# Sixteen filter taps of one convolution tile as diagonal products on TensorE, and the decay factors of two units made on ScalarE

## The chip, the cores and the metric

One core of one Trainium2 chip runs the kernel. The metric is the device time of one execution in microseconds, and the time of a kernel is the median of its runs. PE is TensorE, DVE is VectorE, ACT is ScalarE, SP is the queue that issues most transfers, and PSUM is the memory with eight banks into which PE writes.

## What is computed

One inference step of one decoder layer: a mixer with two groups of heads (an SSD group and a convolution group) that share an input and an output projection, then a mixture of 32 experts with four chosen for each token. There are 272 prompt tokens (16 of them learned, in front) and 8 sample tokens, of width 1024, all in float32. What matters for the change is this part of the mixer:

```python
val, gate = jnp.split(glu_in, 2, axis=-1)
c = val * jax.nn.sigmoid(gate)
c, conf_hist_new = causal_dwconv(c, conf_hist, conv_conf_w, conv_conf_b)   # 31 taps per channel
...
a_cum = jnp.cumsum(dt * a.astype(F32).reshape(g, r), axis=2)
seg = a_cum[:, :, :, None] - a_cum[:, :, None, :]
decay_ls = jnp.exp(jnp.where(causal, seg, -jnp.inf))
cb = jnp.einsum('bclgn,bcsgn->bclsg', cm, bm)
y_diag = jnp.einsum('bclsg,bclsgr,bcsgrp->bclgrp', cb, decay_ls, xdt)
decay_to_end = jnp.exp(a_cum[:, :, -1:] - a_cum)
chunk_decay = jnp.exp(a_cum[:, :, -1])
```

## The kernel before, in words

Channels lie on the 128 partitions, tokens along the free dimension. The order of the work on each engine is the order in which the code is written; semaphores are the only ties between engines.

**PE** makes the input projection in 36 tiles of 128 output channels, each of eight products (`w_in_tiles`, line 1214): 16 for the convolution group, 12 for the SSD group, and 8 Z tiles for the output gate. Z tiles 3 to 7 stand between the steps of the scan. Each tile goes to a PSUM bank that `tile_bank` names, and waits until the bank's former tile has been read; for Z tiles 4 to 7 that is ACT, which applies SiLU to each Z tile (`z_tiles`, line 510, semaphore `z_out`).

**The long convolution** (`wide_conv`, line 696) lies on DVE: eight tiles of 256 tokens with 31 taps each. ACT makes tap 0, and DVE the 30 others, one scalar-multiply-add over a 128x256 tile each, 240 in all. They are dealt out in 90 rounds: rounds 0 to 29 treat tiles 0 and 1 (two taps a round), rounds 30 to 59 tiles 2 and 3, and rounds 60 to 89 tiles 4 to 7, four taps a round. The rounds are laid as filling between steps of other work.

**The scan** handles two chunks of 128 tokens and two groups of eight heads, so four units `u`. For a unit, `exponents` (line 771) subtracts `acum` from the row sums and caps at zero, head by head (eight instructions on DVE), into `Mh[u]`; `decays` (lines 471 and 472) takes the exponential of `Mh[u]` and of the row sums `Ce[u]` on ACT; `unit_factors` (lines 826 to 830) on DVE copies the last column of each to `dec_u` and `cdec_u` and multiplies them by `cbm` and by C. Then PE's `unit` (lines 1257 and 1259) makes the outputs (`y_mm`), waits for `xdec` of DVE (line 852), and makes the new state (line 1263, `st_mm`). DVE waits for `y_mm` at line 861 and for `st_mm` at line 866. Rows of a chunk are transposed by PE (line 1190) and taken over by DVE (`rows_of_chunk`, lines 819 and 821).

**What follows**: after the last round DVE drains and releases `conv_done` (line 870), for which PE waits with the mean of the layer norm (line 1314). Beside this SP loads the output weights once Z tile 7 is done (line 272), the sample states once unit 3's output is done (line 278), and, after DVE's `dtx` has been written to DRAM and is back, its broadcast rows (line 310). DVE's `decode` (lines 875 and 880) uses both, and ahead of the output projection (line 1303) stands the norm (DVE line 901, ACT line 547). The experts follow, with their weights streamed from HBM.

Of the kernel before, what the change touches and what calls it, by code (L numbers as in the profile page):

```python
# [9 lines left out]
ACT = mybir.ActivationFunctionType  # L10
AX = mybir.AxisListType.X

P = 128
D = 1024
KT = D // P
# [32 lines left out]
def build(nc, I, O):  # L48
    ctx = ExitStack()
    with ctx:  # L50
# [52 lines left out]
        Mh = [view(ring, at, HPG, P) for at in (2112, 3136, 12288, 13312)]  # L103
        Ce = [view(ring, 8192 + D * u, HPG, P) for u in range(4)]
# [97 lines left out]
        names = ("rowsum_ready rowsum_out rowsum_landed tap_added narrow_added decay_done consts x_lo x_hi vec_loaded sq_a sq_v stat_mm xr_ready uT_ready win_done gsig_ready glu_done csmp_loaded xsmp_loaded "  # L202
# [27 lines left out]
        def tile_bank(j):  # L230
            if j >= Z_TILE:
                return 4 + j - Z_TILE if j < Z_TILE + 2 else 3 * (j % 2)
            return j % 6
# [187 lines left out]
        def _(a):  # L421
# [47 lines left out]
            def decays(u):  # L469
                a.wait_ge(ev["d_ready"], u + 1)  # L470
                act(flat(Mh[u]), flat(Mh[u]), ACT.Exp).then_inc(ev["e_ready"], 1)
                act(flat(Ce[u]), flat(Ce[u]), ACT.Exp).then_inc(ev["ce_ready"], 1)
# [25 lines left out]
            for x in range(XT_):  # L498
                narrow_first(x)
                if x >= 3 and x % 2:  # L500
                    narrow_silu(x - 3)
                    narrow_silu(x - 2)
# [164 lines left out]
        def _(v):  # L667
# [15 lines left out]
            tap_no = {}  # L683
            for q_ in range(ROUNDS):
                for m_ in CONV_SETS[q_ // NR]:
                    tap_no[m_, 1 + q_ % NR] = len(tap_no) + 1

            def wide_conv(first, last):
                for q in range(first, last):
                    tiles, k = CONV_SETS[q // NR], 1 + q % NR  # L690
                    if k == 1:
                        v.wait_ge(ev["ctap_ready"], tiles[-1] + 1)
                    for m in tiles:
                        if k > 1:
                            v.wait_ge(ev["tap_added"], tap_no[m, k - 1])
                        STT(conv[:, m, 0:SEQ], cbuf[:, m, k:k + SEQ], cw[:, m, k:k + 1], conv[:, m, 0:SEQ], ALU.mult, ALU.add  # L696
                            ).then_inc(ev["tap_added"], 1)
# [115 lines left out]
            exponents(2)  # L813
            exponents(3)

# [7 lines left out]
            def unit_factors(u):  # L823
                c, g_ = u // 2, u % 2
                v.wait_ge(ev["ce_ready"], u + 1)
                V.tensor_copy(dec_u[u], Mh[u][:, :, P - 1])
                V.tensor_copy(cdec_u[u], Ce[u][:, :, P - 1])
                v.drain()
                TT(Mh[u], Mh[u], bc(cbm[:, u, :], 1, HPG), ALU.mult)
                TT(Ce[u], Ce[u], bc(xa[:, 10 + g_, 16 + c * P:16 + (c + 1) * P], 1, HPG), ALU.mult).then_inc(ev["m_ready"], 1)  # L830
# [7 lines left out]
            TT(cbm, ps[:, 4, :].rearrange("p (u t) -> p u t", u=4), bc(tri, 1, 4), ALU.mult)  # L838
# [30 lines left out]
            wide_conv(UNIT_R[3][2], ROUNDS)  # L869
            v.drain().then_inc(ev["conv_done"], 1)  # L870
# [314 lines left out]
        def _(pe):  # L1185
# [12 lines left out]
            def w_in_tiles(first, last):  # L1198
                for j in range(first, last):
# [3 lines left out]
                    if j >= Z_TILE + 4:  # L1203
                        pe.wait_ge(ev["z_out"], j - Z_TILE - 1)
# [60 lines left out]

            w_in_tiles(Z_TILE, Z_TILE + 3)
# [14 lines left out]
            w_in_tiles(Z_TILE + 4, Z_TILE + 5)  # L1281
            unit(0)
            chunk_rows(2, META + P, P)
            w_in_tiles(Z_TILE + 5, Z_TILE + 6)
            unit(1)
            w_in_tiles(Z_TILE + 6, Z_TILE + 7)
            unit(2)
            w_in_tiles(Z_TILE + 7, Z_TILE + 8)
            unit(3)
# [484 lines left out]
```

## Time and profile before

| | us |
|---|---|
| median of 3 runs | 1303.73 (1300.33 to 1305.13) |
| profiled execution, its own time | 1293.74 |
| its span in the trace | 1291.9 |
| busy in the span: PE, DVE, ACT | 1165.0, 495.7, 184.7 |

The span is what the trace covers; 1.8 us of the profiled execution lie around it. "Busy" is an average over stages with different limits, so the stages are what has to be read: the mixer ends at about 300 us, and the remaining 992 us are the experts. A row of a timeline gives the start in us, the time from the first start to the last end of the merged instructions, the engine, line, operation, operands, their count, and in brackets how long the engine was idle before and what released it. Each matmul in float32 shows as two records.

### The profile page before, as it was taken

To read this page: it belongs to the slowest core of one execution; us is meant where nothing else is said; L and a number is where in the kernel's file an instruction comes from. 1 tells how busy PE (TensorE), PEld (TensorE's weight loads), DVE (VectorE), ACT (ScalarE), POOL (GpSimd) and SP (SyncE) were. 2 spreads that over 40 slices of the span, in tenths; PEclk is the share of its full clock that TensorE was granted. 3 is DMA by queue.
4 is the path that set the end of the run, shared out by engine and by line. 5 is a ranking of instruction groups with operands and counts; after the bars stand their busy time and mean duration, and the time that the engine had idled before them with its cause. 6 is when DMAs were issued, how large, how long until landed. Compare 5 with 4: busy or idle time off the path is not lost.

```text
span 1291.9 us, 21086 instructions
## 1 busy us (share of the span) xinstructions
PE 1165.0 (90%) x8422; PEld 547.0 (42%) x8423; DVE 495.7 (38%) x1117; ACT 184.7 (14%) x391; POOL 4.6 (0%) x28
## 2 busy tenths in 40 slices
PE   7999878997998989999989999899999887989886
PEld 5888657873333333333333433233433323323323
DVE  2799998303423322133322232322232332323233
ACT  2132304012111110011100011100111111101011
POOL 0000000000000000000000000000000000000000
PEclk9999988998989999999999999999999999989897
DMA  9541309723799999899999899998999999999993
GB/s 395 200 178 65 139 3 328 280 123 143 308 427 425 428 429 429 324 421 429 429 428 417 332 421 430 429 427 360 395 420 428 430 428 428 428 429 429 428 428 154
DMA packets 36995, 451.33 MB, mean 349 GB/s; under 512 B 5112, under 2 KB 5656, under 8 KB 10080
## 3 DMA queue, kind: packets, MB, share of 16 engines
q1 hardware_dynamic: 35344, 449.02, 83.4%
q10 hardware_dynamic: 1616, 1.82, 0.4%
q8 instruction: 25, 0.41, 0.1%
q14 instruction: 10, 0.08, 0.0%
HBM read 443.57 MB, written 7.25 MB: 349 GB/s over the span
## 4 chain that ended last, share of the span: by engine, by line
PE 57%; DMA 28%; DVE 12%; issue 2%; DVEq 1%; ACT 0%; SPq 0%; ACTq 0%
DMA ring<-in_w_experts 27%; PE ps L1419 24%; PE ps L1462 9%; DVE acts L696 6%; PE ps L1214 3%; PE ps L1303 2%; PE ps L1396 2%; PE ps L1360 2%; PE ps L1429 2%; PE ps L1471 2%; PE ps L1190 2%; DVE acts L791 1%; PE ps L1294 1%; PE ps L1409 1%; PE ps L1452 1%
## 5 line engine op out<-in xcount | busy, mean ns | idle before, releaser
L1419 PE MATMUL ps<-ring,extra 128*64 128x512 f32 x1824 | 418.4, 603 | 13.8 <-DMA ring<-in_w_experts 13.8
L1053 DVE TENSOR_TENSOR acts<-ps,acts 128x528 f32<-128x528 f32 x128 | 90.6, 708 | 398.7 <-PE ps L1429 200.2
L1462 PE MATMUL ps<-ring,extra 128*32 128x256 f32 x3072 | 204.7, 403 | 40.4 <-DMA ring<-in_w_experts 38.1
L1419 PEld LDWEIGHTS ps<-ring,extra 128*64 128x64 f32 x1824 | 123.0, 137 | 262.8 <-issue 232.3
L1462 PEld LDWEIGHTS ps<-ring,extra 128*32 128x32 f32 x3072 | 90.8, 114 | 144.9 <-DMA ring<-in_w_experts 57.4
L696 DVE SCALAR_TENSOR_TENSOR acts<-acts,small 128x256 f32<-128x256 f32 x240 | 97.8, 482 | 0.7 <-ACT acts L451 0.7
L1214 PE MATMUL ps<-acts,ring 128*128 128x280 f32 (+1 forms) x320 | 76.4, 398 | 0.0
L1214 PEld LDWEIGHTS ps<-acts,ring 128*128 128x128 f32 x320 | 61.7, 194 | 15.1 <-issue 2.1
L1214 PE MATMUL ps<-acts,extra 128*128 128x280 f32 x256 | 62.7, 408 | 1.9 <-DVE acts L681 1.9
L1067 DVE TENSOR_SCALAR extra<-ps 128x512 f32<-128x512 f32 x32 | 22.0, 689 | 97.7 <-PE ps L1419 82.4
L1396 PE MATMUL ps<-acts 128*64 128x512 f32 (+1 forms) x228 | 56.6, 616 | 0.0
L1214 PEld LDWEIGHTS ps<-acts,extra 128*128 128x128 f32 x256 | 49.6, 194 | 14.5 <-issue 2.3
L590 ACT ACTIVATE extra<-extra 128x512 f32<-128x512 f32 x32 | 19.7, 630 | 237.1 <-DVE extra L1058 237.1
L1190 PE MATMUL ps<-small,extra 128*128 128x128 f32 x220 | 38.9, 290 | 14.4 <-DVE extra L1072 13.0
L1429 PE MATMUL ps<-acts,extra 64*128 64x264 f32 x304 | 51.1, 426 | 0.0
L1090 DVE SCALAR_TENSOR_TENSOR acts<-ps,acts 128x264 f32<-128x264 f32 x48 | 22.2, 490 | 63.3 <-ACT acts L620 63.1
L1471 PE MATMUL ps<-acts,extra 32*128 32x264 f32 x256 | 46.2, 437 | 0.0
L1190 PEld LDWEIGHTS ps<-small,extra 128*128 128x128 f32 x220 | 22.8, 140 | 48.6 <-issue 20.8
L585 ACT ACTIVATE extra<-ps 128x512 f32<-128x512 f32 x34 | 20.4, 601 | 152.7 <-PE ps L1396 142.0
L1040 DVE TENSOR_SCALAR extra<-ps 128x256 f32<-128x256 f32 x16 | 6.8, 424 | 91.7 <-PE ps L1462 91.7
L1471 PEld LDWEIGHTS ps<-acts,extra 32*128 32x128 f32 x256 | 19.3, 184 | 53.4 <-issue 53.4
L600 ACT ACTIVATE extra<-ps 128x512 f32<-128x512 f32 x32 | 17.4, 594 | 129.4 <-PE ps L1419 129.4
(284 smaller groups left out, 870.4 us busy)
## 6 DMA issues: line engine op xcount, KB each, us to landing
ring<-in_w_experts SPq DMA_DIRECT2D x192, 2048.0 KB, 21.6
ring<-in_w_in_t SPq DMA_DIRECT2D x5, 2048.0 KB, 20.8
extra<-in_w_in_t SPq DMA_DIRECT2D x4, 2048.0 KB, 10.4
extra<-in_w_out_t SPq DMA_DIRECT2D x4, 1024.0 KB, 6.2
ring<-in_w_out_t SPq DMA_DIRECT2D x4, 1024.0 KB, 5.9
ring<-in_state_t SPq DMA_DIRECT2D x8, 512.0 KB, 8.1
ring<-dtx_rows SPq DMA_DIRECT2D x8, 512.0 KB, 6.3
out_ssm_s_t<-ring SPq DMA_DIRECT2D x8, 512.0 KB, 5.2
```

The costliest lines, as they stand in the source:

```text
L696: STT(conv[:, m, 0:SEQ], cbuf[:, m, k:k + SEQ], cw[:, m, k:k + 1], conv[:, m, 0:SEQ], ALU.mult, ALU.add).then_inc(ev["tap_added"], 1)
L1053: TT(both, ps[:, 6:8, 0:TN], both, ALU.add).then_inc(ev["acc_done"], 1)
L1090: return STT(Pm[:, bank, :], ps[:, 6, 0:TN], slot_id[:, slot:slot + 1], gp, ALU.is_equal, ALU.mult)
L1190: return nc.tensor.transpose(out, in_, ident[0:r, 0:r])
L1214: h = MM(ps[:, tile_bank(j), 0:T - lo], win(c)[:, k, P * q:P * (q + 1)], uT[:, k, lo:T], start=(k == 0), stop=(k == KT - 1))
L1303: h = MM(ps[:, m, 0:TN], wout(4 + k // 2)[:, k % 2, P * m:P * (m + 1)], conv[:, k, :], start=(k == 0), stop=False, skip_group_check=True)
L1360: h = MM(ps[:, m, 0:TN], wout(k // 2)[:, k % 2, P * m:P * (m + 1)], yT[:, k, :], start=False, stop=(k == KT - 1), skip_group_check=True)
L1396: h = MM(dst, S[0:r, j, HALF * b:HALF * (b + 1)], xn[0:r, j, 512 * h_:512 * (h_ + 1)], start=(j == 0), stop=(j == 2))
L1419: hs.append(MM(dst, src[:, o:o + HALF], piece(p)[:, k, 512 * h_:512 * (h_ + 1)], start=(fresh and kk == 0), stop=(kk == KT - 1), skip_grou ...
L1429: h = MM(ps[:, 6 + h_, 0:TN], ys[rows, 512 * b + P * m:512 * b + P * (m + 1)], Pm[rows, b, :], start=(b == 0), stop=(b == n - 1))
L1462: hs.append(MM(dst, src[:, o:o + QUAR], piece(p)[:, k, 256 * q:256 * (q + 1)], start=(fresh and kk == 0), stop=(kk == KT - 1), skip_group_ ...
L1471: h = MM(ps[:, 6 + h_, 0:TN], ys[QUAR * q:QUAR * (q + 1), P * (m % 2):P * (m % 2 + 1)], Pm[QUAR * q:QUAR * (q + 1), 0, :], start=True, sto ...
```

## The change

The last convolution tile (tile 7) keeps taps 1 to 14 on DVE. Its taps 15 to 30 become sixteen products on PE: ACT makes sixteen 128x128 diagonal matrices of the tap weights while the SSD group's convolution runs, PE multiplies each with the shifted 128x256 input and accumulates all in PSUM bank 3, in pieces of 5, 4, 4 and 3 behind Z tiles 4 to 7, and DVE adds the bank to tile 7 at the end, ahead of `conv_done`. So that bank 3 is free, Z tiles 4 to 7 all go to bank 0, and each waits for ACT's reading of the one before it.

`exponents` for units 2 and 3 leave DVE: ACT makes them with Relu in `decays`, eight instructions a unit, and takes the sign into the scale of the exponential. The last columns of all four units are copied on ACT behind the exponentials. `unit_factors` loses its copies and the drain, and multiplies `Ce` first, then `Mh`.

```diff
+        PE_TILE, PE_TAP, PE_TAPS = KT - 1, CW - 16, 16
+        diag = view(ring, 14336, PE_TAPS, P)
...
         def tile_bank(j):
             if j >= Z_TILE:
-                return 4 + j - Z_TILE if j < Z_TILE + 2 else 3 * (j % 2)
+                return (4, 5, 0, 3, 0, 0, 0, 0)[j - Z_TILE]
...
             def decays(u):
-                a.wait_ge(ev["d_ready"], u + 1)
-                act(flat(Mh[u]), flat(Mh[u]), ACT.Exp).then_inc(ev["e_ready"], 1)
-                act(flat(Ce[u]), flat(Ce[u]), ACT.Exp).then_inc(ev["ce_ready"], 1)
+                if u < 2:
+                    a.wait_ge(ev["d_ready"], u + 1)
+                    act(flat(Mh[u]), flat(Mh[u]), ACT.Exp)
+                else:
+                    for k in range(HPG):
+                        act(Mh[u][:, k, :], Ce[u][:, k, :], ACT.Relu, scale=-1.0, bias=acum[:, u // 2, HPG * (u % 2) + k:HPG * (u % 2) + k + 1])
+                    a.drain()
+                    act(flat(Mh[u]), flat(Mh[u]), ACT.Exp, scale=-1.0)
+                act(flat(Ce[u]), flat(Ce[u]), ACT.Exp)
+                a.drain()
+                act(dec_u[u], Mh[u][:, :, P - 1], ACT.Copy)
+                act(cdec_u[u], Ce[u][:, :, P - 1], ACT.Copy).then_inc(ev["ce_ready"], 1)
...
                 narrow_first(x)
+                if x >= XT_ - PE_TAPS // 2:
+                    for j in (2 * (x - XT_) + PE_TAPS, 2 * (x - XT_) + PE_TAPS + 1):
+                        act(diag[:, j, :], ident, ACT.Identity, scale=cw[:, PE_TILE, PE_TAP + j:PE_TAP + j + 1]).then_inc(ev["diag_ready"], 1)
...
-                    for m in tiles:
+                    for m in [t for t in tiles if not on_pe(t, k)]:
...
-            exponents(2)
-            exponents(3)
...
             def unit_factors(u):
                 c, g_ = u // 2, u % 2
                 v.wait_ge(ev["ce_ready"], u + 1)
-                V.tensor_copy(dec_u[u], Mh[u][:, :, P - 1])
-                V.tensor_copy(cdec_u[u], Ce[u][:, :, P - 1])
-                v.drain()
-                TT(Mh[u], Mh[u], bc(cbm[:, u, :], 1, HPG), ALU.mult)
-                TT(Ce[u], Ce[u], bc(xa[:, 10 + g_, 16 + c * P:16 + (c + 1) * P], 1, HPG), ALU.mult).then_inc(ev["m_ready"], 1)
+                TT(Ce[u], Ce[u], bc(xa[:, 10 + g_, 16 + c * P:16 + (c + 1) * P], 1, HPG), ALU.mult)
+                v.wait_ge(ev["cbm_ready"], 1)
+                TT(Mh[u], Mh[u], bc(cbm[:, u, :], 1, HPG), ALU.mult).then_inc(ev["m_ready"], 1)
...
             wide_conv(UNIT_R[3][2], ROUNDS)
+            v.wait_ge(ev["taps_mm"], 1)
+            v.wait_ge(ev["tap_added"], tap_no[PE_TILE, PE_TAP - 1])
+            TT(conv[:, PE_TILE, 0:SEQ], conv[:, PE_TILE, 0:SEQ], ps[:, 3, 0:SEQ], ALU.add)
             v.drain().then_inc(ev["conv_done"], 1)
...
                     if j >= Z_TILE + 4:
-                        pe.wait_ge(ev["z_out"], j - Z_TILE - 1)
+                        pe.wait_ge(ev["z_out"], 3 if j == Z_TILE + 4 else j - Z_TILE)
...
+            def pe_taps(first, last):
+                if first == 0:
+                    pe.wait_ge(ev["z_out"], 4)
+                    pe.wait_ge(ev["diag_ready"], PE_TAPS)
+                for j in range(first, last):
+                    h = MM(ps[:, 3, 0:SEQ], diag[:, j, :], cbuf[:, PE_TILE, PE_TAP + j:PE_TAP + j + SEQ],
+                           start=(j == 0), stop=(j == PE_TAPS - 1), skip_group_check=True)
+                return h
...
             w_in_tiles(Z_TILE + 4, Z_TILE + 5)
+            pe_taps(0, 5)
             unit(0)
             chunk_rows(2, META + P, P)
             w_in_tiles(Z_TILE + 5, Z_TILE + 6)
+            pe_taps(5, 9)
             unit(1)
             w_in_tiles(Z_TILE + 6, Z_TILE + 7)
+            pe_taps(9, 13)
             unit(2)
             w_in_tiles(Z_TILE + 7, Z_TILE + 8)
+            pe_taps(13, PE_TAPS).then_inc(ev["taps_mm"], 1)
             unit(3)
```

On DVE, from the end of the SSD group's convolution to the first unit's factors, this stands before (771 is `exponents`, 696 the taps, 826 to 830 `unit_factors(0)`):

```order
L811 TENSOR_TENSOR acts<-acts,small 128x12x8
L771 TENSOR_SCALAR ring<-ring,small 128x128 x16
L696 SCALAR_TENSOR_TENSOR acts<-acts,small 128x256 [waits tap_added] x4
L819 TENSOR_TENSOR ring<-ps,small 16x512 [waits xtok_mm]
L819 TENSOR_TENSOR ring<-ps,small 16x512
L821 COPY ring<-ps 16x256
L836 TENSOR_TENSOR ring<-ring,small 16x1024 [waits meta_exp]
L838 TENSOR_TENSOR small<-ps,small 128x512 [waits cb_mm]
L826 COPY small<-ring 128x8 [waits ce_ready]
L827 COPY small<-ring 128x8
L829 TENSOR_TENSOR ring<-ring,small 128x1024
L830 TENSOR_TENSOR ring<-ring,acts 128x1024
```

and this with the change (713 is the taps, 840 and 842 `unit_factors(0)`):

```order
L828 TENSOR_TENSOR acts<-acts,small 128x12x8
L713 SCALAR_TENSOR_TENSOR acts<-acts,small 128x256 [waits tap_added] x3
L833 TENSOR_TENSOR ring<-ps,small 16x512 [waits xtok_mm]
L833 TENSOR_TENSOR ring<-ps,small 16x512
L835 COPY ring<-ps 16x256
L848 TENSOR_TENSOR ring<-ring,small 16x1024 [waits meta_exp]
L850 TENSOR_TENSOR small<-ps,small 128x512 [waits cb_mm]
L840 TENSOR_TENSOR ring<-ring,acts 128x1024 [waits ce_ready]
L842 TENSOR_TENSOR ring<-ring,small 128x1024 [waits cbm_ready]
```

Sixteen instructions, one tap and two copies are gone from this piece; the rest keeps its order but for the two products of `unit_factors`.

On PE, behind unit 2, this stands before (1214 is Z tile 7, 1257 and 1259 are unit 3's output, 1263 its state, 1190 transposes, 1314 the mean):

```order
L1263 MATMUL ps<-ring 128x512 [waits hT_ready,xdec_ready]
L1214 MATMUL ps<-acts,ring 128x264 [waits z_out]
L1214 MATMUL ps<-acts,ring 128x264 x7
L1257 MATMUL ps<-ring 64x128 [waits hT_ready,y_ready,m_ready,xdt_ready]
L1257 MATMUL ps<-ring 64x128
```

and this with the change (1229 is Z tile 7, 1286 the taps, 1272 the start of unit 3's output):

```order
L1278 MATMUL ps<-ring 128x512 [waits hT_ready,xdec_ready]
L1229 MATMUL ps<-acts,ring 128x264 [waits z_out]
L1229 MATMUL ps<-acts,ring 128x264 x7
L1286 MATMUL ps<-acts,ring 128x256 x3
L1272 MATMUL ps<-ring 64x128 [waits hT_ready,y_ready,m_ready,xdt_ready]
L1272 MATMUL ps<-ring 64x128
```

Three of the sixteen new products now stand between Z tile 7 and unit 3; the other thirteen stand in the same way behind Z tiles 4, 5 and 6.

On ACT, between Z tile 3's SiLU and Z tile 4's, two loads of a table and four exponentials of 128x1024 (lines 471 and 472) stood before; now it is this (477 is the Relu, 479 and 480 the exponentials, 482 and 483 the copies, 524 the SiLU of Z tiles 4 to 7):

```order
L477 ACTIVATE ring<-ring,small 128x128 x8
L479 ACTIVATE ring<-ring 128x1024
L480 ACTIVATE ring<-ring 128x1024
L482 ACTIVATE small<-ring 128x8
L483 ACTIVATE small<-ring 128x8
L477 ACTIVATE ring<-ring,small 128x128 x8
L479 ACTIVATE ring<-ring 128x1024
L480 ACTIVATE ring<-ring 128x1024
L482 ACTIVATE small<-ring 128x8
L483 ACTIVATE small<-ring 128x8
L428 ACT_TABLE_LOAD
L524 ACTIVATE ring<-ps 128x264 [waits win_done] x4
```

Sixteen Relu and four copies have come in ahead of the SiLU of Z tile 4, and nothing there waits for DVE any more.

## Rows read from the trace of the kernel before

**Rows 1.** Windows: busy us (instructions) of PE, PEld, DVE, ACT, POOL; granted clock, DMA share, GB/s.

```profile
57.00:140.00 83.00, 82.28 (x352) 66.48 (x350) 82.67 (x214) 24.37 (x66) 0.24 (x1) 1.00 0.40 149
140.00:201.00 61.00, 43.22 (x267) 32.83 (x268) 58.24 (x138) 10.43 (x15) 0.00 (x0) 0.87 0.21 82
300.00:1292.00 992.00, 894.08 (x7059) 330.08 (x7059) 289.72 (x615) 113.55 (x242) 0.00 (x0) 0.97 0.94 397
```

**Rows 2.** Waits, 137 to 260 us: engine, line, releaser: us in total, times, longest.

```profile
PE ps L1257 <- DVE ring L821: 5.0, 1, 5.0
PE ps L1263 <- DVE ring L852: 4.9, 2, 2.7
PE ps L1314 <- DVEq L870: 4.5, 1, 4.5
PE ps L1278 <- DVE ring L836: 3.1, 1, 3.1
DVE ring L866 <- PE ps L1263: 0.8, 1, 0.8
DVE acts L861 <- PE ps L1259: 0.8, 1, 0.8
```

**Rows 3.** Timeline of DVE in the scan.

```profile
141.31 3.30 DVE L771 TENSOR_SCALAR ring<-ring,small 128x128 f32<-128x128 f32 x16
...
154.67 0.42 DVE L821 COPY ring<-ps 128x256 f32<-128x256 f32 x1
155.00 0.16 DVE L826 COPY small<-ring 128x8 f32<-128x8 f32 x1
...
155.31 1.23 DVE L829 TENSOR_TENSOR ring<-ring,small 128x1024 f32<-128x1024 f32 x1
...
197.21 3.25 DVE L696 SCALAR_TENSOR_TENSOR acts<-acts,small 128x256 f32<-128x256 f32 x8
```

**Rows 4.** Timeline of PE: unit 0, a state, a Z tile, a variance.

```profile
157.51 0.44 PE L1257 MATMUL ps<-ring 128*64 128x128 f32 x4
...
159.09 0.39 PE L1259 MATMUL ps<-ring 128*64 128x128 f32 x4
...
161.68 1.13 PE L1263 MATMUL ps<-ring 128*128 128x512 f32 x2 [2.20 <-DVE ring L852]
...
188.63 3.73 PE L1214 MATMUL ps<-acts,ring 128*128 128x264 f32 x16
...
206.78 3.62 PE L1319 MATMUL ps<-acts,small 128*128 128x256 f32 x16
```

**Rows 5.** Timeline of ACT.

```profile
84.61 0.60 ACT L451 ACTIVATE acts<-acts,small 128x256 f32<-128x256 f32 x1 [0.86 <-DVE acts L706]
...
86.53 0.28 ACT L476 ACTIVATE small<-ps 128x128 f32<-128x128 f32 x1
...
146.47 1.28 ACT L426 ACT_TABLE_LOAD   x1
147.76 1.06 ACT L471 ACTIVATE ring<-ring 128x1024 f32<-128x1024 f32 x1
```

**Rows 6.** Windows of PE alone: busy us (records), granted clock, DMA share, GB/s.

```profile
159.00:162.00 3.00, 0.80 (x11) 1.00 0.00 0
169.00:171.50 2.50, 0.36 (x8) 1.00 0.00 0
171.50:175.00 3.50, 2.96 (x5) 0.51 0.00 0
182.00:188.50 6.50, 5.35 (x34) 0.50 0.00 0
```

**Rows 7.** Timeline behind the scan: output weights, mean, broadcast rows, first decode.

```profile
192.39 0.81 SPq L272 DMA_DIRECT2D ring<-in_w_out_t  x2
...
200.65 6.29 PE L1314 MATMUL ps<-acts,small 128*128 128x264 f32 x16 [4.47 <-DVEq L870]
...
207.23 1.76 SPq L310 DMA_DIRECT2D ring<-dtx_rows  x4
...
211.19 1.41 DVE L880 SCALAR_TENSOR_TENSOR ring<-ring,acts 128x512 f32<-128x512 f32 x2 [0.65 <-DMA ring<-dtx_rows]
```

More of the change, by code:

```diff
@@ L199, in build @@
         lgT = view(acts, 5016, TN)
-        names = ("rowsum_ready rowsum_out rowsum_landed tap_added narrow_added decay_done consts x_lo x_hi vec_loaded sq_a sq_v stat_mm xr_ready uT_ready win_done gsig_ready glu_done csmp_loaded xsmp_loaded "
+        names = ("cbm_ready diag_ready taps_mm rowsum_ready rowsum_out rowsum_landed tap_added narrow_added decay_done consts x_lo x_hi vec_loaded sq_a sq_v stat_mm xr_ready uT_ready win_done gsig_ready glu_done csmp_loaded xsmp_loaded "
                  "dt_mm dt_v dt_exp dt_ready ctap_ready conv_done xtap_ready xtail_out xconv_done xs_pre xa_ready z_out "
@@ L683, in _, with on_pe @@
             tap_no = {}
+            def on_pe(m, k):
+                return m == PE_TILE and k >= PE_TAP
             for q_ in range(ROUNDS):
-                for m_ in CONV_SETS[q_ // NR]:
+                for m_ in [t for t in CONV_SETS[q_ // NR] if not on_pe(t, 1 + q_ % NR)]:
                     tap_no[m_, 1 + q_ % NR] = len(tap_no) + 1
@@ L837, in _ @@
             v.wait_ge(ev["cb_mm"], 1)
-            TT(cbm, ps[:, 4, :].rearrange("p (u t) -> p u t", u=4), bc(tri, 1, 4), ALU.mult)
+            TT(cbm, ps[:, 4, :].rearrange("p (u t) -> p u t", u=4), bc(tri, 1, 4), ALU.mult).then_inc(ev["cbm_ready"], 1)
             unit_factors(0)
```

## The prediction

> **What bounds the kernel now.** I began with the windows by stage [rows 1]. From 57 to 140 us DVE is busy 82.67 of 83 us, from 140 to 201 us 58.24 of 61, while PE has 43.22 of 61 and a clock of 0.87 on average, and ACT 10.43. So up to the end of the scan DVE is the bound. Behind 300 us the transfers are (0.94 busy); the change touches nothing there. The list of waits [rows 2] says the same from the other side: in the scan it is PE that waits for DVE, 5.0 us at unit 2, 4.9 us for two states, 3.1 us for the first state's factors and 4.5 us for `conv_done`. DVE waits for PE only twice, 0.8 and 0.8 us, both in unit 2. The reader is to see that an instruction taken from DVE in this stretch moves the end of the scan, and that one given to PE first fills a pause.
>
> The clock matters here [rows 6]. Unit 2 runs at 0.50, that is 1.2 GHz, after the pause of 5.0 us before it. The pause before the state at 161.68 was 2.20 us and the clock stayed at 1.00 (2.4 GHz); a pause of 2.7 us later [rows 2] was followed by 0.51. So a pause of 2.2 us has left the clock high once, one of 2.7 us has not.
>
> **The change part by part.**
>
> *Exponents of units 2 and 3.* Sixteen instructions leave DVE: 3.30 us from first start to last end [rows 3], of which 3.2 us are its own, since the next starts a little ahead of an end. Gain 3.2 us.
>
> *Taps.* Eight taps take 3.25 us from first start to last end, and each goes on 0.395 us behind the former [rows 3]. Sixteen leave: 6.3 us. They are one in the last step of the SSD convolution, one before the first rows, and fourteen inside the scan. With three tiles a round a tap still has two others between itself and its predecessor; with two tiles a round, early in the kernel, DVE was full as well [rows 1], so no new pause arises.
>
> *Copies and drain.* From the first copy (155.00) to the product (155.31) are 0.31 us [rows 3], four times: 1.2 us. The new waits on `ce_ready` and `cbm_ready` are looked at with ACT below; `cbm` is DVE's own work, one product earlier.
>
> *The addition at the end.* Not in the trace. Nearest are the copy of 128x256 from PSUM, 0.42 us, and half of the 128x1024 product's 1.23 us, 0.6 us [rows 3]. I take 0.4 and keep 0.6 as the upper end; it cannot gain. PE has made `taps_mm` before unit 3, whose output DVE has waited for, so it never waits.
>
> Sum on DVE: 3.2 + 6.3 + 1.2 - 0.4 = 10.3 us.
>
> *Sixteen products on PE.* A product of 128x256 is two of the sixteen records that take 3.62 us, so 0.43 us [rows 4]. Sixteen are 6.9 us. At half the clock it is 0.86 us, and that is the other bound; below 0.43 it will not be, since the shape is the same. Follow PE: the 3.1 us pause before the first state vanishes, because its factors are ready 4 us earlier and Z tile 3 ends later than they do. From there to unit 2 PE is nearly without a pause: in unit 0 the five products (2.2 us) and the output (157.51 to 159.48, 1.97 us [rows 4]) end before `xdec` is wanted, and unit 1 with four (1.7 us) ends some 2.7 us before DVE asks for it. Before unit 2 it waits for the rows of chunk 2, now about 1.8 us instead of 5.0 (the four products fill 1.7, and the earlier DVE takes the rest). That is shorter than the 2.20 us that left the clock high. I take the high clock for unit 2. Then its output takes 1.97 and its state 1.13 us instead of 3.7 and 2.0, and both waits of DVE in unit 2 end: a gain of 1.6 us that is no part of the DVE sum.
>
> In unit 3 the opposite happens. From the end of unit 2's state PE has Z tile 7 (3.73 us), three products (1.3) and the output (1.97): 7.0 us. DVE from there: it reaches the state about 0.4 us later (it now comes second), then 0.6 for line 866, six taps 2.4, `xdec` and `hT2` 1.3, three taps 1.2: 5.9 us. DVE waits 1.0 us.
>
> Sum at `conv_done`: 10.3 + 1.6 - 1.0 = **10.9 us**.
>
> *ACT.* The sixteen diagonals stand in a stretch where ACT is busy 24.37 of 83 us [rows 1], each behind the `narrow_first` that DVE waits for: hidden. If that cover were gone each pair would cost about 0.6 us. The decays of units 2 and 3 start with the table at about 146.0 + 0.1 us. A Relu of 128x128 with one operand per partition is not in the trace. Above lies 0.60 us for 128x256 with two such operands, below 0.28 for 128x128 with none [rows 5]; I take 0.37 alone and 0.28 in a row (an overlap of 0.09, as DVE's instructions at 154.67 and 155.00 show [rows 3]). Eight are 2.3 us, two exponentials 2.0 (1.06 the first), copies and drains 0.4: 4.7 us a unit. So unit 2 is ready at 147.4 + 4.7 = 152.1, unit 3 at 156.8; DVE asks for them at about 158 and 167 on the new time: it came to them at 163.7 and 174.1, and has by then gained 3.2 (exponents), 0.6 and 0.9 (copies) and five and eight taps (2.0 and 3.2). Then the table (1.28) and Z tile 4's SiLU (0.4) end at 158.5, and PE wants bank 0 for Z tile 5 at 158.8: from the end of Z tile 3 (145.9) two first states 1.8, transposes 1.1, Z tile 4 3.7, five products 2.2, unit 0's 1.97 and 1.13, transposes 1.1. This fits just; behind it lie the 2.7 us by which unit 1 is early. At 0.51 us a Relu (the 0.60 row less the overlap) it ends 3.7 us later, PE is late by 3.4, and DVE loses 1 to 1.6 us. Z tiles 6 and 7 find the bank long free: they are 8 us or more apart and SiLU takes 0.4.
>
> The Trainium skill speaks against this move: "ScalarE: Activation LUTs", section "Rules for kernel authors", tells to use VectorE for relu, max and min. Per instruction the trace agrees, 3.2 us on DVE against some 4.5 on ACT. By that rule alone the move would lose 1.3 us; by the rows it wins 3.2, because ACT has the time and DVE hasn't.
>
> *Does it reach the end?* `conv_done` is one way into the tail, the transfers the other. The broadcast rows were issued at 207.23, after `dtx` came back from DRAM behind the output weights (from 192.39) and the states, and DVE's first decode waited 0.65 us for them at 211.19 [rows 7]. That queue starts when Z tile 7 is done. With the change Z tile 7 ends at about 181.4 instead of 192.3: DVE has the rows of chunk 2 ready 8.4 us earlier (3.2, copies 1.2, ten taps 4.0), and unit 2 at the high clock saves 2.6. So this way moves by about 11 us too. Both move alike, and everything behind hangs on them in order; expert weights are first fetched when the states are done. So 10.9 us arrive. The mean at 200.65 took 6.29 us for the sixteen records after a 4.47 us pause; at the high clock it would take about 3.5. The pause will be some 2.5 us. Either way the decode behind it waits for the rows, so this gives only 0 to 0.65 us, and I take 0.
>
> **Sum**: 1293.74 - 10.9 = 1282.8 us for an execution like the profiled one, -0.84%. That execution was 0.8% faster than the median of the runs, 1303.73; the same share off the median gives **1292.8 us**.
>
> **Rivals.**
> 1. *PE becomes the bound.* If the clock stays low through the products (0.86 us each, units at 3.7), PE is late in units 1, 2 and 3 by 0.9, 2.0 and 2.7 us. For it speaks the mean clock of 0.87 and 0.51 after short pauses [rows 1, 6]; against it, that all its pauses become shorter. The gain falls to about 6.4 us: 1297.3. Chance 0.12. (Only unit 2 low: 9.2 us of gain, 1294.5, within the forecast.)
> 2. *The tail gives more.* The mean is at 2.4 GHz and the rows' transfers, less crowded, come earlier as well. Up to 2.8 us more: 1290.0. For it, the 2.5 us pause lies between the two seen; against it, the 0.65 us wait. Chance 0.14.
> 3. *The gain does not reach the end.* Something behind 300 us, where transfers are 0.94 busy for 992 us [rows 1], starts at a time the mixer does not set. Against it: the weights' first fetch waits for the sample states. 1303.7. Chance 0.08.
> 4. *Slower: ACT holds bank 0.* The two units' sixteen Relu stand ahead of Z tile 4's SiLU, for which Z tile 5 waits, and unit 1 and all taps behind it wait with it. PE may be late 2.7 us for free; the sign turns when the delay exceeds 2.7 + 10.9 = 13.6 us, that is 0.85 us more per Relu, 1.1 us each. At 1.3 us each it is 2.7 us slower: 1306.5. No row of 128 columns comes near [rows 5]. Chance 0.04.
> The forecast itself holds 0.62.
>
> **Numbers.** About 0.5% (6.5 us, below 1297.2) is what a measurement tells from no change. The forecast with its bounds (addition 0.2, Relu 1.6, unit 2's clock 1.7) is 1292.5 to 1296.5, and the runs of before spread by 2.5 us around their median; with rivals 1 and 2 in it the range is 1289 to 1298. Faster: 0.62 + 0.14 + half of rival 1 = 0.82; same 0.06 + 0.08 = 0.14; slower 0.04.
>
> **What the new profile would show.** DVE without line 771's sixteen in the scan and taps in threes and sixes; no pause of PE before the first state; no wait of DVE in unit 2 and about 1.0 us for `y_mm` in unit 3; products of 0.43 us; Relu of about 0.28 us apart; Z tile 5 hardly waiting for `z_out`; `conv_done` near 189.6. The forecast is wrong if a Relu takes over 0.5 us, if DVE waits for PE in units 1 and 2, or if the first broadcast rows land less than 10 us earlier.

## The result, and the profile after

| | before | after |
|---|---|---|
| median of the runs taken together | 1304.43 us (4) | 1286.84 us (4) |
| lowest to highest | 1300.33 to 1305.66 | 1283.26 to 1288.3 |
| profiled execution: time, span | 1293.74, 1291.9 | 1288.3, 1286.5 |

The ratio is 0.9873, with a 95% interval of 0.9845 to 0.9901: the kernel is 1.3% faster, by 17.6 us in these medians of four. The forecast of 1292.8 us (1289 to 1298) had the direction and missed the size; the median lies 2.2 us below the range. The two profiled executions differ by 5.4 us only, so the first question is where each stands among its kind.

The windows by stage of after, as in [rows 1], cut at the start of the scan, at `conv_done` and at 300 us:

```profile
57.00:141.50 84.50, 84.46 (x368) 68.31 (x366) 82.25 (x213) 29.22 (x85) 0.24 (x1) 1.00 0.42 158
141.50:191.10 49.60, 44.13 (x298) 34.45 (x298) 48.16 (x99) 16.27 (x36) 0.00 (x0) 1.00 0.25 95
191.10:300.00 108.90, 101.16 (x529) 82.77 (x531) 44.79 (x100) 27.14 (x57) 2.35 (x12) 0.93 0.63 237
300.00:1286.00 986.00, 895.17 (x7041) 327.12 (x7037) 284.07 (x588) 110.84 (x233) 0.00 (x0) 0.96 0.94 397
```

The scan takes 49.6 us where it took 61.0, DVE is still the bound in it (48.16 busy), and PE's clock is 1.00 from end to end, where it was 0.87.

The waits from 130 to 260 us, to be held against [rows 2]:

```profile
DVE ring L895 <- DMA ring<-dtx_rows: 3.2, 1, 3.2
...
PE ps L1342 <- DVEq L885: 2.7, 1, 2.7
...
PE ps L1272 <- DVE ring L835: 1.9, 1, 1.9
...
DVE acts L873 <- PE ps L1274: 0.7, 1, 0.7
...
PE ps L1229 <- ACT ring L524: 0.3, 1, 0.3
```

PE's four rows in [rows 2] add up to 17.5 us; in the same places, with Z tile 5 added, 4.9 are left. The wait before the first state and those for `xdec` are gone, the one before unit 2 went from 5.0 to 1.9 us, the one for `conv_done` from 4.5 to 2.7. (Behind `conv_done` PE has a new wait of 1.6 us in all, for DVE's decode.) DVE no longer waits in unit 2 and waits 0.7 us in unit 3 (forecast 1.0). Z tile 5 waited 0.3 us for bank 0 (forecast: it just fits).

The timelines of DVE, PE and ACT in the scan, for [rows 3 to 5]:

```profile
143.11 1.27 DVE L713 SCALAR_TENSOR_TENSOR acts<-acts,small 128x256 f32<-128x256 f32 x3
...
172.68 2.46 DVE L713 SCALAR_TENSOR_TENSOR acts<-acts,small 128x256 f32<-128x256 f32 x6
...
186.55 1.12 DVE L873 SCALAR_TENSOR_TENSOR acts<-acts,small,ps 128x128 f32<-128x128 f32 x4 [0.72 <-PE ps L1274]
...
190.58 0.42 DVE L884 TENSOR_TENSOR acts<-acts,ps 128x256 f32<-128x256 f32 x1
```

```profile
154.38 2.32 PE L1286 MATMUL ps<-acts,ring 128*128 128x256 f32 x10
...
161.03 3.83 PE L1229 MATMUL ps<-acts,ring 128*128 128x264 f32 x16 [0.29 <-ACT ring L524]
...
191.17 3.80 PE L1342 MATMUL ps<-acts,small 128*128 128x264 f32 x16 [2.73 <-DVEq L885]
```

```profile
149.57 2.45 ACT L477 ACTIVATE ring<-ring,small 128x128 f32<-128x128 f32 x8
152.09 1.06 ACT L479 ACTIVATE ring<-ring 128x1024 f32<-128x1024 f32 x1
```

Taps come in threes and sixes, the addition (L884) takes 0.42 us, and no `exponents` stand in the scan. Five products take 2.32 us, 0.46 each with the overlap. Eight Relu take 2.45 us, 0.30 apart. The mean (L1342) takes 3.80 us instead of 6.29, at a granted clock of 1.00.

The tail on DVE, for [rows 7]:

```profile
197.34 1.22 DVE L890 TENSOR_TENSOR ring<-ring,small 128x1024 f32<-128x1024 f32 x1
201.73 1.41 DVE L895 SCALAR_TENSOR_TENSOR ring<-ring,acts 128x512 f32<-128x512 f32 x2 [3.17 <-DMA ring<-dtx_rows]
```

The wait for the broadcast rows grew from 0.65 to 3.17 us: what the mean gave, this wait took.

### The profile page after: what moved, and what is told of

The parts are those of the page before. It is cut to its first block, busy times and chain, and to the rows that moved or that the text cites. A ratio compares the mean times of both kernels' runs of the same rounds, so it can differ in the third digit from the quotient of the medians.

```text
span 1286.5 us, 21155 instructions
## 1 busy us (share of the span) xinstructions
PE 1173.8 (91%) x8454; PEld 551.2 (43%) x8455; DVE 485.5 (38%) x1078; ACT 195.5 (15%) x431; POOL 4.6 (0%) x28
## 4 chain that ended last, share of the span: by engine, by line
PE 55%; DMA 30%; DVE 12%; issue 1%; DVEq 1%; ACT 0%; SPq 0%; ACTq 0%
DMA ring<-in_w_experts 29%; PE ps L1447 24%; PE ps L1490 8%; DVE acts L713 5%; PE ps L1229 3%; PE ps L1331 2%; PE ps L1424 2%; PE ps L1388 2%; PE ps L1499 2%; PE ps L1457 2%; PE ps L1205 2%; DVE acts L808 1%; PE ps L1322 1%; PE ps L1437 1%; PE ps L1480 1%
## 5 line engine op out<-in xcount | busy, mean ns | idle before, releaser
L1447 PE MATMUL ps<-ring,extra 128*64 128x512 f32 x1824 | 426.3, 613 | 15.3 <-DMA ring<-in_w_experts 15.3
L713 DVE SCALAR_TENSOR_TENSOR acts<-acts,small 128x256 f32<-128x256 f32 x224 | 91.3, 477 | 0.7 <-ACT acts L453 0.7
L1082 DVE TENSOR_SCALAR extra<-ps 128x512 f32<-128x512 f32 x32 | 22.0, 688 | 97.8 <-PE ps L1447 82.5
L1424 PE MATMUL ps<-acts 128*64 128x512 f32 (+1 forms) x228 | 56.6, 616 | 0.0
L1457 PE MATMUL ps<-acts,extra 64*128 64x264 f32 x304 | 51.2, 427 | 0.0
```

What stands on the lines that cost most here:

```text
L1424: h = MM(dst, S[0:r, j, HALF * b:HALF * (b + 1)], xn[0:r, j, 512 * h_:512 * (h_ + 1)], start=(j == 0), stop=(j == 2))
L1447: hs.append(MM(dst, src[:, o:o + HALF], piece(p)[:, k, 512 * h_:512 * (h_ + 1)], start=(fresh and kk == 0), stop=(kk == KT - 1), skip_grou ...
L1457: h = MM(ps[:, 6 + h_, 0:TN], ys[rows, 512 * b + P * m:512 * b + P * (m + 1)], Pm[rows, b, :], start=(b == 0), stop=(b == n - 1))
```

## Stages of all traces

To see where executions differ I took six marks in each trace: the start of the scan (DVE's 128x384 product, 141.43 in after), the 128x64 product behind `conv_done` (191.11), DVE's first addition of the output projection (255.82), the first and the last gate of the experts with few tokens, and the last output. "Start" is the time of DVE's first copy of the row sums. The table gives the distances in us, and under it every experiment refers to it. The last column gives the span. The columns do not add up to it: from "start" to the scan it is 82.9 us in before and 82.5 in after, and from the last gate to the end 35 to 37.

| trace | start | scan | to the projection's first sum | to the first gate | experts | span |
|---|---|---|---|---|---|---|
| before, the one shown | 56.7 | 61.0 | 63.4 | 90.4 | 900.7 | 1291.9 |
| before, again | 56.5 | 60.9 | 65.7 | 94.4 | 900.5 | 1297.9 |
| before, a third | 58.9 | 60.8 | 66.2 | 96.6 | 903.6 | 1304.8 |
| before, a fourth | 56.5 | 60.9 | 63.9 | 91.7 | 901.1 | 1292.6 |
| after, the one shown | 58.9 | 49.7 | 64.7 | 91.8 | 902.0 | 1286.5 |
| after, again | 56.4 | 49.7 | 65.4 | 91.7 | 900.5 | 1282.3 |
| after, a third | 56.8 | 49.7 | 65.1 | 92.1 | 901.9 | 1283.3 |
| decays only | 56.8 | 55.2 | 62.9 | 91.7 | 900.0 | 1285.4 |
| taps only | 56.8 | 56.1 | 65.9 | 91.9 | 901.2 | 1290.0 |
| products unread | 56.2 | 61.0 | 66.5 | 92.0 | 901.3 | 1295.7 |
| four times Relu | 56.1 | 64.7 | 66.6 | 92.1 | 901.5 | 1298.9 |
| after + 1.1 us | 56.8 | 49.9 | 64.4 | 93.4 | 901.1 | 1282.9 |
| after + 2.0 us | 56.4 | 49.7 | 63.1 | 93.6 | 900.1 | 1284.2 |
| after + 3.4 us | 56.9 | 51.2 | 66.3 | 100.7 | 900.9 | 1297.2 |
| before + 1.3 us | 59.0 | 62.6 | 65.7 | 94.4 | 900.1 | 1301.8 |
| before + 2.65 us | 56.1 | 59.4 | 62.4 | 91.7 | 901.5 | 1292.1 |
| before + 3.4 us | 56.5 | 60.8 | 63.1 | 90.4 | 898.6 | 1291.9 |
| after, filled | 56.6 | 49.7 | 65.4 | 90.2 | 899.0 | 1279.2 |
| before, filled | 55.3 | 62.4 | 67.7 | 89.6 | 902.2 | 1296.4 |
| after + 1.1, filled | 56.9 | 49.9 | 66.7 | 91.5 | 899.4 | 1285.4 |

In the four traces of before and the three of after the scan is 60.8 to 61.0 and 49.7 us: 11.1 to 11.3 us shorter whichever two are compared. On the mean the spans differ by 12.8 us: 11.2 in the scan, 0.4 ahead of it, 1.2 from the scan's end to the first gate, and nothing in the experts. That last stretch goes with PE's granted clock in it: in before it took 153.8, 155.6, 160.1 and 162.8 us at a clock of 0.94, 0.93, 0.90 and 0.90, in after 156.5, 157.1 and 157.2 us at 0.93, 0.92 and 0.92.

Before's scan is not always the same, though. "Before, filled" has its edit behind the scan and yet a scan of 62.4 us. In it the clock fell already in the products of the first state (0.53 from 148 to 152 us), and DVE waited 1.44 us for the rows of chunk 1. PE in before, then PE and DVE in "before, filled":

```profile
149.16 1.95 PE L1278 MATMUL ps<-ring 16*128 16x512 f32 x4 [3.13 <-DVE ring L836]
```

```profile
147.78 3.32 PE L1278 MATMUL ps<-ring 16*128 16x512 f32 x4 [3.14 <-DVE ring L836]
...
153.46 1.29 DVE L819 TENSOR_TENSOR ring<-ps,small 128x512 f32<-128x512 f32 x2 [1.44 <-PE ps L1190]
```

## Experiments

**Both kernels again**, with more executions.

> The kernel before, unchanged, as a control. Open question: the medians of before and after lie 17.6 us apart, but 10.9 us were forecast and the two traces show 11.2 us less from the sample convolution (before 139.71, after 141.51 us) to the end of the wide convolution, and their spans differ by 5.4 us only. Theory A (variation): executions of one kernel differ by several us outside the scan (clock at the start, expert stage), the extra 6.7 us is such variation, and this control comes out within 3 us of the kernel before with a scan of 60.8 us in its trace. Theory B (real): the scan before normally takes longer than in the one trace shown (pauses fall differently against the clock), so that this trace, if its time is near 1303, shows the scan 4 to 8 us longer than 60.8 us.

> The changed kernel, unchanged, timed in more rounds. Theory A: the difference to before shrinks towards 11 us (8 to 14). Theory B: it stays at 15 to 20 us.

Measured: before 1300.9 us (12 executions, 1295.56 to 1306.62), after 1285.4 (6, 1284.09 to 1288.02), 0.9898 [0.9849, 0.9947] against the runs of before beside it. Against the 1299.6 of before beside it, after is 14.2 us faster, between the 8 to 14 of theory A and the 15 to 20 of theory B; the scan of before is 60.9 us in its trace, so the long scan of theory B did not show. The first median of before was high by chance: 123 executions of it beside the experiments have a median of 1299.98, from 1291.22 to 1310.41; 16 of after have 1286.15, from 1283.26 to 1291.45. The difference is thus about 13.8 us, not 17.6 (95% of the differences lie between 12.6 and 15.8 when both sets of executions are drawn anew, with repetition, many times).

**Each half alone.** The one kernel is after without `on_pe`, diagonals, `pe_taps` and the bank table; the other is after with the decays as before:

```diff
-                return m == PE_TILE and k >= PE_TAP
+                return False
```

```diff
+            exponents(2)
+            exponents(3)
...
+                V.tensor_copy(dec_u[u], Mh[u][:, :, P - 1])
+                V.tensor_copy(cdec_u[u], Ce[u][:, :, P - 1])
+                v.drain()
```

> Only the decay part: exponents of units 2 and 3 and the copies of all units on ACT, all thirty taps of tile 7 on DVE, banks as before. By the sum of the prediction DVE loses 3.2 and 1.2 us of work: the end of the wide convolution 4.4 us earlier, and up to 2.6 us more if unit 2 runs at 2.4 GHz (its pause stays near 5 us, so I expect 1.2 GHz there): 1299 to 1300 us. Theory B: 6 us or more.

> Only the taps: sixteen products on PE, exponents and copies stay on DVE. By the sum: 6.3 less 0.4 us of DVE work, 1.6 us if unit 2 comes to run at 2.4 GHz (its pause falls to about 2.8 us), 1.0 us lost in unit 3: 5 to 7 us, 1297 to 1299. Theory B: 9 us or more.

Measured: decays alone 1293.04 (0.9967 [0.993, 1.0004]), taps alone 1293.07 (0.995 [0.9917, 0.9982]). Their scans are 5.8 and 4.9 us shorter, 10.7 together; both at once give 11.3. In medians they give some 7 us each against 1299.98, and 13.8 together. Both times lie below their ranges by the sum (1299 to 1300, 1297 to 1299), but the median of before was still uncertain, and the interval of decays alone reaches from no gain to 9 us: that each half gives more than its scan is not shown. With taps alone DVE waits 1.63 us for the rows of chunk 1, which are late at a low clock as in "before, filled". With decays alone PE still waits 6.1 us before unit 2, and unit 2 meets the low clock, as was expected: its first four records take 0.69 us, where they take 0.44 in after:

```profile
178.58 0.69 PE L1269 MATMUL ps<-ring 128*64 128x128 f32 x4 [6.10 <-DVE ring L835]
```

By the Trainium skill ("ScalarE: Activation LUTs", section "Rules for kernel authors", use VectorE for relu) `exponents` belongs on DVE. Per instruction the traces agree: 0.20 us apart on DVE [rows 3], 0.30 on ACT. The stage decides otherwise: with this half alone, copies included, the scan is 5.8 us shorter, because DVE was busy for 58.24 of 61 us and ACT for 10.43 [rows 1].

**The products alone.** Before, with the diagonals and the sixteen products in their places, while DVE makes all taps itself and nobody reads bank 3:

```diff
             w_in_tiles(Z_TILE + 4, Z_TILE + 5)
+            pe_taps(0, 5)
             unit(0)
```

> The kernel before, in which ACT also makes the sixteen diagonals and PE the sixteen products in their new places, with the new banks, but DVE still adds all taps itself and reads none of the products. DVE has the same work as before. What the products can do here is fill PE's pauses. Clock theory (the extra gain is that PE no longer falls to 1.2 GHz in the scan, and that this fall varies from run to run before): faster than before by 1.5 to 5 us, no DVE wait in unit 2, and runs that spread less than before's 19 us. Plain sum theory (all gain is DVE work removed, the rest of the difference lies behind the scan by chance): no change or up to 1.3 us slower, and the spread of before.

Measured: 1299.62, 0.9985 [0.9961, 1.0009], scan 61.0, as by the plain sum theory. The products cost nothing and bring nothing that can be told from noise: some 7 us of PE's work lie in pauses. PE still waits 4.67 us before unit 2, and the clock in the scan is 0.89 instead of 0.87; with the taps gone from DVE it is 0.91, with both halves 1.00.

**Relu four times over**, to see whether ACT can hold bank 0 (rival 4):

```diff
+                    for _ in range(4):
+                        for k in range(HPG):
+                            act(Mh[u][:, k, :], Ce[u][:, k, :], ACT.Relu, ...)
```

> The changed kernel with the eight Relu of units 2 and 3 done four times each (same result, a drain behind each pass), so that ACT reaches the SiLU of Z tile 4 about 14.8 us later. By the rival on ACT: PE waits some 15 us for the bank at Z tile 5, 2.7 us of that free, and the scan grows by 12 us, from 49.7 to about 62, the time of before or a little more. If Z tile 5 were not what matters, but only the decays themselves, units 2 and 3 would have them 7.4 and 14.8 us later against leads of about 5 and 9 us: 5 to 6 us lost.

Measured: 1303.4, 1.0023 [0.9996, 1.0049], scan 64.7: all of the gain is lost. The timeline of PE shows the chain that rival 4 describes, and that of DVE who pays. (DVE also waits 2.04 and 3.39 us for the late decays of units 2 and 3, but behind these it still waits for PE, so the bank sets the end.)

```profile
173.32 5.71 PE L1230 MATMUL ps<-acts,ring 128*128 128x264 f32 x16 [15.37 <-ACT ring L525]
```

```profile
182.71 1.12 DVE L874 SCALAR_TENSOR_TENSOR acts<-acts,small,ps 128x128 f32<-128x128 f32 x4 [8.74 <-PE ps L1275]
```

The 48 added Relu are 14.6 us (0.305 each, from the eight in 2.45), and rival 4 put the turn of the sign at 13.6: with a median just above before's, that fits. Its mechanism is real; only the Relu is not slow. Its price was too low: the scan grew by 15.0 us where 12 were expected, and behind the pause the Z tile took 5.71 us instead of 3.83, at a clock of 0.70 from 173 to 180 us.

**Single traces of before.** Two more of them, so that its spread can be seen by stage.

> The kernel before, one more look. The 29 runs of before spread from 1291 to 1310 us, the changed kernel's from 1283 to 1288. If the scan causes the spread, a run over 1303 shows it longer than 61 us with half clock in units 0, 1 or 3; if not, the scan is 61 us again and the difference lies in the experts or in their start.

> The same once more, for a second point: scan 61 us whatever the time, or longer with the time.

Measured: 1306.62 and 1294.43. The table shows 12.2 us of span between them, and none in the scan: 2.4 at the start, 2.3 ahead of the projection's first sum, 4.9 ahead of the first gate, 2.5 in the experts. Two groups of eight products behind the routing, and a window of PE alone, in the slower:

```profile
327.86 3.68 PE L1419 MATMUL ps<-ring,extra 128*64 128x512 f32 x8
...
332.65 3.68 PE L1419 MATMUL ps<-ring,extra 128*64 128x512 f32 x8
320.00:330.00 10.00, 9.01 (x38) 0.65 0.01 2
```

and in the faster:

```profile
322.50 1.94 PE L1419 MATMUL ps<-ring,extra 128*64 128x512 f32 x8
...
325.01 1.94 PE L1419 MATMUL ps<-ring,extra 128*64 128x512 f32 x8
320.00:330.00 10.00, 10.00 (x54) 0.94 0.00 0
```

The same instructions take 3.68 us in the one and 1.94 in the other.

**Delays.** One, two or three unread products with a drain on DVE ahead of the scan. They move all that follows. If stages add up, each costs its length. The runs are named by what the way from "start" to the scan grew by in their traces (1.1 and 2.0 for the 1.0 and 1.75 that were planned, 1.3 and 2.65 for 1.2 and 2.4; in the two called 3.4 it grew by 3.6). What the expectations call the grid are the moments at which the clock was seen to change in the traces.

```diff
             exponents(1)
             v.drain()
+            TT(flat(cprod)[:, 0:870], flat(csmp)[:, 0:870], flat(csmp)[:, 0:870], ALU.mult)
+            v.drain()
```

> The changed kernel with one more DVE product and a drain of about 1.0 us in all, ahead of the SSD convolution, so that everything from the scan on starts 1.0 us later and nothing else changes. Where the clock may change is a grid of moments that does not follow the kernel: in ten traces all changes of one run lie on one grid, and the grid lies elsewhere in each run, but the start of the kernel draws the work to within 1.1 us of it. Grid theory: the later stages cost more or less by where they fall on the grid. 11.2 us less in the scan put them at a cheap place; 1.0 us more puts them where the kernel before has them, so this kernel is 3 to 5 us slower than the changed kernel, not 1.0 (ratio to before 0.992 instead of 0.989), and its runs spread over 10 us or more instead of 4 to 5. Chance theory (the changed kernel's time is just 11 us less, and ten runs were luckily low): 1.0 us slower.

> The changed kernel with 1.75 us more at the same place. Grid theory: between, slower by something other than 1.75 us, most likely by 2 to 6, with a wide spread, for the decays-only kernel (5.7 us less in the scan, whose later stages lie about there) spread over 16 us. Chance theory: 1.75 us slower.

> The kernel before with 1.2 us more at the same place. Chance theory: 1.2 us slower. Grid theory: anything from 2 us faster to 5 slower; together with the other three it gives the cost over the grid.

> The kernel before with 2.4 us more of DVE work at the same place. Grid theory: this puts the later stages of the kernel before on the cheap place of the changed kernel, so it is not slower than before (from 1 us faster to 0.5 slower), and its runs spread over about 5 us instead of 16 to 19. Chance theory: 2.4 us slower (ratio 1.002), same spread.

> The changed kernel with 3.4 us more of DVE work ahead of the SSD convolution (the runs with 1.1 and 2.0 us more were 5.3 and 7.5 us slower on the mean). [...] Theory that added work costs a multiple of itself: 9 to 12 us slower, 1295 us or more, and wide.

> The kernel before with 3.4 us more at the same place. [...] Multiple theory: slower by 6 us or more.

> The changed kernel unchanged, as the base of the same session: 1284 to 1288 us and a spread of 4 to 5 us if its ten narrow runs were no luck; if they were, 1285 to 1295 with a spread of 10 us or more.

| kernel | median us (lowest to highest) | against 1286.15 or 1299.98 |
|---|---|---|
| after + 1.1 | 1291.18 (1284.76 to 1298.04) | +5.0 |
| after + 2.0 | 1295.14 (1283.15 to 1301.92) | +9.0 |
| after + 3.4 | 1292.46 (1286.87 to 1299.33) | +6.3 |
| after, a third time | 1285.92 (1285.25 to 1291.45) | -0.2 |
| before + 1.3 | 1302.07 (1297.68 to 1310.29) | +2.1 |
| before + 2.65 | 1302.89 (1293.78 to 1308.41) | +2.9 |
| before + 3.4 | 1297.54 (1293.69 to 1304.76) | -2.4 |

In after all three cost more than their length: 1.1 us cost 5.0 in the median (4.5 in the mean, by drawing anew from the executions between 1.9 and 7.0), and the spread grew from 8 to 13 us. In before 1.3 and 2.65 us cost about their length, within a noise of some 3 us, and 3.4 us cost less than nothing. I had expected the place of a stage against the moments at which the clock can change to foretell these. It did so for the first (after + 1.1). After + 2.0 was wide, as expected, but slower than expected in the median. Before + 2.65 was to be no slower and narrow, and was wide; either kernel + 3.4 was to cost 3.4 us, and they cost 6.3 and -2.4, which is below what the multiple theory expected too. For before + 1.3 nothing definite had been expected. In after + 3.4 a part of the reason shows: the delay opened a pause of PE of 3.21 us ahead of the scan, and the clock fell right behind it, as the timeline and the windows of PE show:

```profile
143.65 1.54 PE L1211 MATMUL ps<-small,acts 128*16 128x128 f32 x10 [3.21 <-ACT acts L506]
```

```profile
144.00:148.00 4.00, 4.00 (x21) 0.57 0.01 4
```

**The routing pause filled.** In the routing PE waits for DVE's mask with nothing to do, and the clock falls. Four unread products of 128x512 in that pause and one behind the next step:

```diff
+            for _ in range(4):
+                MM(ps[:, 5, :], ident, vecs[:, 0:512], start=True, stop=True)
             pe.wait_ge(ev["mask_ready"], 1)
...
             h.then_inc(ev["pos_mm"], 1)
+            MM(ps[:, 5, :], ident, vecs[:, 0:512], start=True, stop=True)
```

> The kernel after, and PE makes four unread products of 128x512 before it waits for the routing mask and one behind the positions, so that its pause there (4.35 us in the trace of the third run of after) is filled. If the clock in the routing stage is what the stages behind the scan differ by: granted clock 0.9 or more from 290 to 310 us, the way from the output projection to the first expert 88 to 90 us instead of 92.1, time 2 to 4 us below after (about 1283), and its executions lie within 3 us. If the clock there is not what costs (the transfers are): way and time unchanged (92, 1286). If the unread products stand in the way: 1 to 3 us slower.

> The same five unread products in the kernel before. If the clock in routing is what makes the executions of before spread by 15 to 19 us and their median lie 3 us higher than the scan explains: median 4 to 6 us below before, spread under 10 us. If the spread comes from elsewhere (the clock before the scan, or behind its end): median 0 to 4 us lower, spread as it was.

> The kernel after with 1.1 us more on DVE ahead of the scan (which cost 5.3 us without the unread products) and the same five unread products. If the 4 us beyond the 1.1 came from the clock in routing: 1.1 us above the filled kernel, within 1.5 us. If they came from elsewhere: 4 to 6 us above it.

Measured: after filled 1282.15 (1280.76 to 1285.05), 0.9868 [0.9823, 0.9913] against before; before filled 1297.96 (1290.64 to 1301.66), 0.9966 [0.9936, 0.9995], 3.7 us below the 1301.69 of before beside it; after + 1.1 filled 1285.13 (1282.91 to 1287.18). The routing stage of after in its third trace, windows and timeline of PE:

```profile
290.00:295.00 5.00, 2.80 (x16) 0.61 1.01 433
295.00:300.00 5.00, 3.48 (x11) 0.50 0.48 134
```

```profile
292.20 0.63 PE L1410 MATMUL ps<-acts,small 128*128 128x32 f32 x2 [4.35 <-DVE acts L968]
297.28 4.89 PE L1524 MATMUL ps<-acts 128*64 128x512 f32 x12 [1.52 <-DVE acts L989]
```

and filled:

```profile
290.00:295.00 5.00, 4.27 (x24) 1.00 1.03 439
295.00:300.00 5.00, 4.53 (x34) 1.00 0.46 141
```

```profile
287.88 3.70 PE L1407 MATMUL ps<-small 128*128 128x512 f32 x8
292.31 0.41 PE L1412 MATMUL ps<-acts,small 128*128 128x32 f32 x2 [0.73 <-DVE acts L968]
...
295.94 2.94 PE L1527 MATMUL ps<-acts 128*64 128x512 f32 x12 [0.47 <-DVE acts L989]
```

The same twelve records take 2.94 us instead of 4.89 and end 3.3 us earlier. Filling this pause gives 4.0 us in after and 3.7 in before, the same within a noise of some 2 us, so the clock in it is not what the two kernels were seen to differ by. For after this is what the first theory expected, but the way to the first gate is 90.2 us (88 to 90 expected), the clock fell later instead (0.74 from 305 to 310 us), and the executions lie within 4.3 us, not 3. For before the second theory fits: 3.7 us, and a spread of 11.0 us where it was 16.0 beside it. The delay of 1.1 us cost 3.0 filled, between the two expectations and with too few executions to tell it from 5.0. After filled is the fastest kernel here: 4.0 us below the pooled after, 1.3% below before.

## Why the prediction was wrong

**What bounds the kernel, and the scan: right.** Every step has its row. Exponents, copies and taps left DVE as counted; the addition took 0.42 (0.4); a Relu is 0.30 apart (0.28); unit 2 ran at the high clock, with its two DVE waits gone; the wait in unit 3 was 0.72 (1.0). The sum at `conv_done` was 10.9 us. The scan is 11.3 us shorter (61.0 to 49.7), and one of the sixteen taps stands ahead of its first mark, where the way from "start" fell from 82.9 to 82.5 us: 11.7 us in all, 0.8 more than forecast, of which 0.3 are the shorter wait in unit 3; the rest has no row. `conv_done` was forecast for 189.6 and came at 191.1, behind a start of the scan that was 1.8 us later (141.4 instead of 139.6), which is not the change's: one of before's traces has the same start of 58.9.

**The tail.** "Either way the decode behind it waits for the rows, so this gives only 0 to 0.65 us, and I take 0": right, and the rows show it twice, the mean at 3.80 us and the 3.17 us of waiting behind. Measured from the scan's start, the first decode came 11.3 us earlier (60.3 instead of 71.6). On the trace's own clock it is 9.5 us (211.19 to 201.73), less than the 10 us that were named as a sign of being wrong, but the later start makes up the 1.8. Rival 2, that the tail gives more by itself, is thus not what happened, though its time of 1290.0 was nearer. Rival 1 fell (clock 1.00 through the scan), rival 3 too.

**The step that failed most** is the conversion to a median: "the same share off the median gives 1292.8 us". It set out from 1303.73, the median of three executions, 3.7 us above the 1299.98 of many. From 1299.98 the same sum gives 1289.1 us, and a range moved with it (1285.3 to 1294.3) holds the 1286.8 that was measured. The range failed by the same step: it took 2.5 us for what executions of before differ by, from those three, while 137 of them lie within 19.2 us. That was to be read beforehand: the profiled execution lay 10 us below the median, so executions of one kernel differ by 10 us at least, and a median of three could be off by several. The 17.6 us of the first result hold the same chance: 13.8 us, and 3.8 because both medians were of four.

**The second step that failed** is "Both move alike, and everything behind hangs on them in order; [...] So 10.9 us arrive". The order is as said, but the stages behind are not of fixed length. They hold PE pauses, and the clock behind each varies from one execution to the next: `conv_done` to the first sum takes 63.4 to 66.2 us in before, and from there to the first gate 90.4 to 96.6. In medians 13.8 us arrive, 2.1 more than the 11.7 at `conv_done`; drawing anew from the executions puts this surplus between 0.9 and 4.1. The three terms add up: 1292.8 less 3.7 for the base, less 0.8 at `conv_done`, less 2.1 behind it gives the 1286.2 of the pooled after.

The surplus is in keeping with the clock. Over 137 executions of before the mean granted clock is 0.958, over the 16 of after 0.967. Of this 0.009 some 0.006 are the scan's own (0.87 to 1.00 over 61 of 1292 us), which the 11.7 us already hold; 0.003 are left. Among the executions of before 0.001 of clock goes with 0.91 us of time (r = -0.81), so 0.003 would be 2.7 us, an estimate. Before's executions at 0.964 to 0.968 have a mean of 1295.0, those below 0.956 one of 1305.9. After has fewer of the long ones: its 16 lie within 8.2 us, before's 137 within 19.2.

**What stays open.** The cause of the surplus of some 2 us is not shown. In the traces 1.2 us of it lie between `conv_done` and the first gate and go with the clock there; but before's scan was also 62.4 us once, at an unchanged scan, so a part can lie in the scan itself, where after gave 49.7 us in all four traces with an unchanged scan. Why after would meet the low clock less often is open: the delays did not come out as the place of the stages foretold, and filling one pause took about 4 us from both kernels and left their distance at 15.8 us (1297.96 to 1282.15). Pauses ahead of the first sum and behind the routing stage were not filled.

## What to carry to other kernels

Read what a stage gives from its timeline, but take the base from many executions, and if the profiled one lies far from the median let the range hold that distance. Where PE pauses stand behind the stage that is changed, the stages behind need not keep their length, so that single microseconds don't always add up (in after 1.1 cost 5.0); a few unread products in one pause of 4.35 us brought 4 us. An instruction that is dearer on an idle engine still wins when it leaves the engine that bounds the stage, and the turning point is the slack of whatever waits behind it, here bank 0.

## What the runs showed of the hardware

- The same program's start differs by 2.4 us: in the three traces with a late start (58.9 and 59.0) PE's granted clock is 0.91 over the first 20 us, in the others (55.3 to 56.9) 1.00.
- PE pauses of 1.90 and 2.73 us in after were followed by a clock of 1.00 (the scan, and the mean in 3.80 us), one of 2.7 us in before by 0.51 [rows 2, 6], one of 4.35 us by 0.50. In before + 2.65 one of 3.36 us, ahead of unit 2, was followed by 1.00 as well. The length of a pause alone did not tell, near 3 us, which way it goes.
- A write of 32 KB (`dtx`, issued at 192.49) was back for the next issue at 197.74, 5.2 us later; in before it was 5.3 us (201.97 to 207.23). Output weights and states were in transfer beside it.
